# Sample attention with stationary queries, column groups, softmax in halves, and gathered values

## The chip, the core and the metric

The kernel runs on one core of one Trainium2 chip. Its time is the device time of one execution in microseconds (us). TensorE (PE) multiplies; VectorE (DVE), ScalarE (ACT) and GpSimd (POOL) work on tiles; SyncE (SP) issues transfers only, and POOL and ACT issue some too. Each has its own in-order queue, and the queues meet in semaphores.

## What is computed

One layer of a hybrid decoder runs for a prompt of 512 tokens and for a sample group of 8 sequences with one new token each and 2048 tokens behind them. This is the reference of the sample group's attention, which the change rewrites, cut to what matters (B = 8, 8 query heads in 2 key heads of 64, pages of 128 rows, 16 pages to a sequence):

```python
def nsa_sample(a_q, a_kv, a_gate, pool_kc, pool_vc, pool_ks, pool_vs, win_k, win_v, page_table, ...):
    q, (kcr, vcr, ksr, vsr, kwr, vwr) = split_nsa(a_q, a_kv)
    kc = compress(full_rows(pool_kc, kcr), cmp_pe[0], cmp_w1[0], cmp_w2[0])   # 127 rows of 32 tokens
    vc = compress(full_rows(pool_vc, vcr), cmp_pe[1], cmp_w1[1], cmp_w2[1])
    o_cmp, p_grp = cmp_attend(q, kc, vc, q_pos)                  # softmax; p summed over 4 heads
    tok = block_tokens(select_blocks(p_grp, q_pos, PAST_LEN + Q))  # the best 16 of 33 blocks of 64
    o_sel = gathered_attend(q, gather_paged(pool_ks, ...), gather_paged(pool_vs, ...), tok, q_pos)
    o_win = band_attend(q, kw, vw, q_pos, ...)                   # the last 512 rows and the new one
    return combine_branches(a_gate, o_cmp, o_sel, o_win)         # sigmoid gates, sum of three
```

After the three branches the layer computes `merged = sum_b sigmoid(x Wg_b) * (y_b @ w_branch_b)`. Branch 1 of this sum is the attention's.

## The kernel before

The program is a chain of phases: norm, RWKV, mLSTM, prompt attention, sample attention (class `Sample`, from L1603), merge, and feed-forward. All engines meet at a phase's end (`meet`, L247). Everything is fp32, and each matmul in the program is two instructions on TensorE, here called passes. Weights come in pieces of 128 columns through a ring of four (`PIECES`, `weights_in`, L2246); `product` (L238) and `part` (L228) multiply a piece with all 520 tokens.

**One sample.** The 16 pages of a sample lie in one of two buffers, `PG[b % 2]`; a page is 128 x 384 floats: the raw rows of the compressed branch for keys and for values, and the selected branch's keys. SP issues the even pages and POOL the odd ones (`key_pages`), each after reading the page's number into a register. Both wait for the scores of the sample two earlier, `s_sc_ps(b - 2)`, since these were the buffer's last readers. POOL waits for the queries, `qd`, ahead of everything else of the phase; SP fetches samples 0 and 1 a phase ahead. On TensorE the sample is this: L1627 compresses the pages (16 matmuls of 256 columns, 32 passes); L1635 scores the compressed keys of two samples earlier; L1647 shifts and adds the two halves of the blocks of one sample earlier; L1655 scores the selected keys:

```python
for pg in range(NPAGE):
    ins = nc.tensor.matmul(PS[:, 2, pg * 8:pg * 8 + 8], p_[:, pg, 2, :], QD[:, b, :], start=True, stop=True)
```

Here a page's keys are the stationary operand, and the 8 columns of `QD`, one for each head, move. L1659 does the same with the window's keys, and L1669 and L1672 finish the compressed keys and values, `KCs` and `VCs`. VectorE copies all scores into `SC_`, 23 slots of 64 columns (8 samples x 8 heads), with the keys on the partitions.

**After the last sample.** One softmax over all samples follows for the compressed branch (`softmax`, L1676 to L1683 on TensorE: a transpose of the maxima, a broadcast product, a sum), then the ranking of the blocks (L1689, L1692), a mask spread over the keys by 16 products with the constant `BSEL` (L1697), the softmax of the selected and then of the window's scores, and one gate product of the merge (L238). The values come by 128 loads of 64 KB (`value_pages`, L1598) on three queues, SP, POOL and ACT, into six buffers of the then free `PG`; a window's values come on SP. Per sample 23 matmuls (L1713 to L1718) take 8 columns of `SC_` as the stationary operand, and 128 columns of values move. L1722 turns the results back.

**Merge.** For each of 8 output tiles m TensorE computes the attention's gate product (8 matmul pairs) and its branch product (4 pairs), ScalarE the sigmoid, and VectorE the product and the sum. The gate of m = 0 is the one computed inside the sample phase.

Of the kernel before, what the change touches and what calls it, by code (L numbers as in the profile page):

```python
# [20 lines left out]
I32 = mybir.dt.int32  # L21
# [15 lines left out]
RING = 4  # L37
CH = 64
# [8 lines left out]
def constants():  # L47
# [22 lines left out]
    n, j = p[:, None], np.arange(NBLK)[None, :]  # L70
    c["covers"] = ((n < 4 * j + 4) & (n >= 4 * j - 1) & (n < 127)) * 1.0
# [4 lines left out]
    c["first"] = np.zeros((128, 1))  # L76
    c["first"][0] = NEG
# [6 lines left out]


def block_selector():

    e = np.zeros((128, NPAGE, 2, 64))
    for b in range(32):
        e[b, b // 2, b % 2] = 1.0  # L90
    return e.reshape(128, 2048)[0:32].astype(np.float32)
# [62 lines left out]
def build(nc, io, known, phases):  # L154
    ctx = ExitStack()
    with ctx:
# [59 lines left out]
        plan("merge", [8, 4] * 8)  # L216
# [1060 lines left out]
        class Attn:  # L1277
# [245 lines left out]
            def pool(p):  # L1523
# [18 lines left out]
        NSLOT = 23  # L1542
        WIN = [Qr[:, i * 512:(i + 1) * 512] for i in range(2)]
        HIDS = take(512)
        HID, HSGs = HIDS[:, 0:256], HIDS[:, 256:512]
        KCs = take(128)
        QD = take(NS * 8).rearrange("p (b h) -> p b h", b=NS)
        SC_ = take(NSLOT * 64).rearrange("p (s n) -> p s n", s=NSLOT)
        VCs = take(NS * 128).rearrange("p (b f) -> p b f", b=NS)
        MXs, SMs = take(192), take(192)  # L1550
        MXT = take(1)
        DGm = take(192)
        GBs = take(192)
        spent = w1d.rearrange("p kv j l h -> p (kv j l h)")
        ONEW = spent[:, 2048:4096].rearrange("p (k b f) -> p k b f", k=2, b=NS)
        BSEL = spent[:, 0:2048].rearrange("p (g n) -> p g n", g=NPAGE)
        OH = spent[:, 0:1024]
        PGRP = take(16)
        RANK, RSEL = take(NBLK), take(NBLK)
        TOP8 = take(8)  # L1560
        ADDT = take(16)
        ADD = take(256).rearrange("p (g n) -> p g n", g=NPAGE)
        G24D = take(192)
        VPw = [ap.rearrange("p (g f) -> p g f", g=4) for ap in (
            Qr[:, 1024:1536], Qr[:, 1536:2048], KVr[:, 0:512], KVr[:, 512:1024], SGe[:, 0:512], HIDS, *WIN)]
# [6 lines left out]
        VP = [PG[i // 3].rearrange("p g k n -> p (g k n)")[:, i % 3 * 2048:(i % 3 + 1) * 2048].rearrange("p (g f) -> p g f", g=NPAGE)  # L1572
              for i in range(NV)]
        assert a <= TOP - 4680, a
        SLOTS = {"sel": (0, 17), "win": (17, 22), "cmp": (22, 23)}
# [15 lines left out]
        def value_pages(queue, b, lane):  # L1591

            if b < NV:
                queue.wait_ge(*at("s_sc_ps", NS - 2 + b // 3))
            else:
                queue.wait_ge(*at("s_pv", b - NV))
# [4 lines left out]
        HALVES = [[ap[:, :] for ap in ST], [XS[:, :], US[:, :]]]  # L1601

        class Sample:  # L1603
            def pe(pe):

                pe.wait_ge(*at("g24d"))
                ins = nc.tensor.matmul(PS[:, 7, 0:192], C("ones")[0:24, :], G24D[0:24, :], start=True, stop=True)
                ins.then_inc(*step("pe", "gb_ps"))

                for i, kv in enumerate((3, 5)):  # L1610
                    for b in range(NS):
# [816 lines left out]
```

## Time and profile before

| what | value |
|---|---|
| time, median of 3 runs | 1775.79 us (1774.44 to 1775.86) |
| the profiled execution | 1774.47 us, its span 1772.8 us |
| TensorE's mean granted clock | 0.92 |
| PE busy | 1577.5 us, 89% |
| PE weight loads busy | 1305.5 us, 74% |
| DVE, ACT, POOL busy | 682.0, 292.4 and 87.4 us |
| sample phase | 243.2 us (941.2 to 1184.4) |
| its share of one sample | about 18 us, eight times |

The engine that is busy longest is TensorE; the shares say little of one phase, though, since each has limits of its own. The rows that matter are those of the sample phase and of what borders on it: TensorE's timeline with the idle time before each group of instructions and what ended it, the granted clock by stretch, and the transfers' issues. A clock of 1.00 is 2.4 GHz, 0.50 is 1.2 GHz.

### The profile page before, as it was taken

What the parts mean: (1) busy time and instruction counts of PE and PEld (TensorE: products, weight loads), DVE (VectorE), ACT (ScalarE), POOL (GpSimd) and SP (SyncE); (2) the same over time, 40 slices, a digit from 0 to 9 for tenths busy, and PEclk for the clock granted to TensorE, in tenths of its full rate; (3) what the DMA queues carried; (4) which work ended last, traced back from release to release, by engine and by line L of the source; (5) the groups of instructions that cost most, each with busy time, mean ns of one, the idle gap of its engine ahead of it and who ended that gap; (6) DMA issues with size and microseconds to landing.
All of it is one profiled execution on the core that took longest, in us unless ns stands there. A gap on an engine that the chain in (4) does not pass through costs nothing.

```text
span 1772.8 us, 26473 instructions
## 1 busy us (share of the span) xinstructions
PE 1577.5 (89%) x11104; PEld 1305.5 (74%) x11104; DVE 682.0 (38%) x1114; ACT 292.4 (16%) x577; POOL 87.4 (5%) x160
## 2 busy tenths in 40 slices
PE   4996699997888698999998997699988999999993
PEld 3874499886666487777767886478877888888883
DVE  3226855335556503433441102301127545554222
ACT  1013101111321001334431011000011111110000
POOL 0000000000000102000002223000000000000000
PEclk9996799998989596999999786799999999999997
DMA  4220000110211247211105563332222222212301
GB/s 152 72 83 25 25 26 16 40 49 16 72 62 36 77 163 156 67 54 54 48 25 167 184 212 121 111 123 78 84 72 80 95 74 93 96 48 99 121 10 49
DMA packets 57082, 143.35 MB, mean 81 GB/s; under 512 B 12050, under 2 KB 31587, under 8 KB 52835
## 3 DMA queue, kind: packets, MB, share of 16 engines
q1 hardware_dynamic: 36722, 97.01, 16.8%
q0 software_dynamic: 14480, 42.02, 7.7%
q10 hardware_dynamic: 5760, 2.62, 0.5%
q8 instruction: 88, 1.44, 0.3%
q14 instruction: 32, 0.25, 0.0%
HBM read 134.11 MB, written 11.65 MB: 82 GB/s over the span
## 4 chain that ended last, share of the span: by engine, by line
PE 84%; DVE 12%; ACT 1%; issue 1%; DMA 1%; POOL 0%; DVEq 0%; SPq 0%; ACTq 0%; POOLq 0%
PE PS L1982 22%; PE PS L238 20%; PE PS L228 11%; PE PS L1627 4%; PE PS L1234 3%; PE PS L1655 2%; PE PS L1713 2%; PE PS L1379 1%; PE PS L254 1%; PE PS L1374 1%; PE PS L1342 1%; PE PS L524 1%; PE PS L536 1%; PE PS L537 1%; PE PS L989 1%
## 5 line engine op out<-in xcount | busy, mean ns | idle before, releaser
L238 PE MATMUL PS<-xyr 128*128 128x260 f32 x1184 | 268.0, 389 | 4.0 <-DVE arena L825 2.5
L238 PEld LDWEIGHTS PS<-xyr 128*128 128x128 f32 x1184 | 228.7, 194 | 40.6 <-DVE arena L825 2.9
L228 PE MATMUL PS<-xyr 128*128 128x260 f32 x896 | 215.3, 393 | 11.0 <-DVE xyr L301 5.8
L228 PEld LDWEIGHTS PS<-xyr 128*128 128x128 f32 x896 | 169.4, 194 | 48.1 <-DVE xyr L301 6.6
L1982 PE MATMUL PS<-arena 128*128 128x260 f32 x638 | 145.1, 383 | 1.5 <-DVE arena L2140 1.3
L1982 PEld LDWEIGHTS PS<-arena 128*128 128x128 f32 x638 | 120.9, 190 | 21.5 <-DVE arena L2140 1.7
L1982 PE MATMUL PS<-xyr 128*128 128x260 f32 x512 | 119.2, 382 | 0.0
L1982 PE MATMUL PS<-arena,xyr 128*128 128x260 f32 x484 | 110.3, 382 | 0.0
L1982 PEld LDWEIGHTS PS<-xyr 128*128 128x128 f32 x512 | 97.3, 190 | 14.9
L1982 PEld LDWEIGHTS PS<-arena,xyr 128*128 128x128 f32 x484 | 92.0, 190 | 14.1
L238 PE MATMUL PS<-arena,xyr 128*128 128x260 f32 x384 | 87.4, 388 | 2.2 <-DVE arena L1920 1.6
L238 PEld LDWEIGHTS PS<-arena,xyr 128*128 128x128 f32 x384 | 73.9, 193 | 14.2 <-DVE arena L1920 2.0
L1627 PE MATMUL PS<-arena 128*128 128x256 f32 x256 | 71.8, 449 | 2.4 <-DVE arena L1769 2.4
L1627 PEld LDWEIGHTS PS<-arena 128*128 128x128 f32 x256 | 58.3, 231 | 13.7 <-DVE arena L1769 2.7
L1520 DVE COPY arena<-PS 128x512 f32<-128x512 f32 x20 | 13.8, 692 | 82.7 <-PE PS L1374 82.7
L2152 DVE TENSOR_TENSOR arena<-PS,arena 128x260 f32<-128x260 f32 x22 | 9.4, 429 | 92.6 <-ACT arena L2082 92.6
L1401 ACT ACTIVATE arena<-PS,arena 128x128 f32<-128x128 f32 (+3 forms) x64 | 32.9, 527 | 56.2 <-DVE arena L1485 56.1
L1982 PE MATMUL PS<-xyr,arena 128*128 128x260 f32 x176 | 42.2, 382 | 0.0
L683 DVE TENSOR_TENSOR arena<-arena 128x512 f32<-128x512 f32 x14 | 9.7, 693 | 76.8 <-ACT arena L601 76.8
L1588 POOL DMA_DIRECT2D arena<-in_pages x64 | 34.4, 538 | 88.2 <-issue 88.2
L537 PE MATMUL PS<-arena 64*64 64x64 f32 x640 | 37.8, 218 | 0.0
L536 PE MATMUL PS<-arena 64*64 64x64 f32 x640 | 37.8, 218 | 0.0
(478 smaller groups left out, 2190.9 us busy)
## 6 DMA issues: line engine op xcount, KB each, us to landing
xyr<-in_w SPq DMA_DIRECT2D x73, 512.0 KB, 3.5
xyr<-in_w_up SPq DMA_DIRECT2D x22, 1024.0 KB, 4.9
arena<-in_pages SPq DMA_DIRECT2D x64, 192.0 KB, 3.6
arena<-in_pages POOLq DMA_DIRECT2D x64, 192.0 KB, 3.8
xyr<-in_w_down SPq DMA_DIRECT2D x10, 704.0 KB, 8.0
xyr<-in_w SPq DMA_DIRECT2D x24, 256.0 KB, 2.7
arena<-in_w_down SPq DMA_DIRECT2D x6, 704.0 KB, 6.0
arena<-in_x POOLq DMA_DIRECT2D x2, 2080.0 KB, 8.6
```

The lines of the kernel that those rows point to most:

```text
L228: ins = nc.tensor.matmul(PS[:, 2 * bank + half, 0:HALF], weight(g, k), XN[:, k, half * HALF:(half + 1) * HALF], start=k == 0, stop=k == KT ...
L238: ins = nc.tensor.matmul(PS[:, 2 * bank + half, 0:HALF], weight(g, k), src[:, k0 + k, half * HALF:(half + 1) * HALF], start=first and k == ...
L254: ins = nc.tensor.matmul(PS[:, 2 * t + half, 0:HALF], C(which), src[:, t, half * HALF:(half + 1) * HALF], start=True, stop=True)
L536: nc.tensor.matmul(PS[q, 4 + g // 8, g % 8 * 64:g % 8 * 64 + 64], TTt[q, g, :], Wt[q, g, :], start=True, stop=True)
L537: ins = nc.tensor.matmul(PS[q, g // 8, g % 8 * 64:g % 8 * 64 + 64], Wt[q, g, :], TTt[q, g, :], start=True, stop=True)
L1234: ins = nc.tensor.matmul(PS[:, 2 * FILL + half, 0:HALF], weight(g, k), src[:, k, half * HALF:(half + 1) * HALF], start=k == 0, stop=k == 3)
L1401: nc.scalar.activation(Pb[i % 2][:, x, 0:W], PS[:, x, 0:W], ACT.Exp, bias=NBi[i % 2][:, x:x + 1], scale=SCALE, accum_out=SUMi[i % 2][:, x: ...
L1588: queue.dma_start(PG[b % 2][:, pg], io["pages"][page(queue, b, pg)].rearrange("a p k n -> p (a k) n")).then_inc(*moved("pages", b, lane, l ...
L1627: ins = nc.tensor.matmul(PS[:, kv, 0:256], w1[:, kv, l, :, :].rearrange("p j h -> p (j h)"), p_[:, :, kv, l * 16:(l + 1) * 16], start=l == ...
L1655: ins = nc.tensor.matmul(PS[:, 2, pg * 8:pg * 8 + 8], p_[:, pg, 2, :], QD[:, b, :], start=True, stop=True)
L1713: nc.tensor.matmul(out, SC_[:, pg, o], VP[b % NV][:, pg, :], start=pg == 0, stop=False)
L1982: ins = nc.tensor.matmul(dst, w[:, k, :], src[:, k, :], start=first and k == 0, stop=k == n - 1, skip_group_check=not first)
```

## The change

It rewrites the sample phase and takes three gates of the merge into it.

- **Queries.** `QZ` holds for each sample 32 columns that are zero but for the 8 heads of its place in its half (samples 0 to 3, 4 to 7). They are the stationary operand now, and the keys move: four products of 512 columns (L1723), each into a column group of its own, partitions 32c to 32c + 31 of the result. The four samples of a half add up in one bank, so that after four samples the 128 partitions hold all scores of the half: 4 page groups x 4 samples x 8 heads. The window (L1727) and the compressed keys (L1661) go the same way.
- **Compressed rows.** Block-diagonal weights `W2B` make keys and values in one product each (L1653, L1654). The new row of a branch is written into column 0 of the window's and the compressed keys, so that no product has a single row. Halves are shifted and added in the same sample (L1737).
- **Softmax in halves.** A row lies on four partitions now, and constants (`mod32`, `rep4`) join them. Half 0 is worked out during samples 4 to 7, a step in the middle or behind a page product each; half 1 between gates and values. VectorE's 32 x 32 block transposes turn the probabilities into the stationary operand `PT` of the value products.
- **Values.** `PT` has 32 columns, the values move in four column groups (L1674). One indirect gather on POOL brings a sample's 16 value pages (1 MB, 128 rows of 2048 floats); the 128 row numbers are worked out on VectorE from a table that POOL loads first. The window's values are loaded on SP between the key pages. ScalarE copies each sample's result and TensorE adds the four groups (L1684).
- **Gates.** The gate products m = 0, 1, 2 stand in the sample phase, cut into parts (`gate_part`), and ScalarE keeps their sigmoids in `GATED`.
- **Constants** are 160 columns wider, and `blocksel` is gone.

```diff
+AHEAD = 3
...
-        plan("merge", [8, 4] * 8)
+        plan("gates", [8] * AHEAD)
+        plan("merge", [4] * AHEAD + [8, 4] * (8 - AHEAD))
...
             if b >= 2:
                 queue.wait_ge(*at("s_sc_ps", b - 2))
-                queue.wait_ge(*at("s_hid_ps", b - 2))
...
-            for pg in (range(0, 6), range(6, 11), range(11, NPAGE))[lane]:
-                queue.dma_start(VP[b % NV][:, pg], io["pages_v"][page(queue, b, pg)].rearrange("a p n -> p (a n)")).then_inc(
-                    *moved("pages_v", b, lane, lane=NV * lane + b % NV))
+            p.indirect_dma_start(VP[b % NV], None, io["pages_v"], bass.IndirectOffsetOnAxis(ap=IDX[:, b:b + 1], axis=0)).then_inc(
+                *moved("pages_v", b, lane=b % NV))
...
+                    for i in range(NPAGE):
+                        c = i % 4
+                        nc.tensor.matmul(PS[32 * c:32 * c + 32, bank_, 0:128], PT[hf][:, i * 32:i * 32 + 32],
+                                         VP[b % NV][:, i * 128:i * 128 + 128], start=i < 4, stop=False)
+                    for c in range(3, -1, -1):
+                        nc.tensor.matmul(PS[32 * c:32 * c + 32, bank_, 0:128], PTw[hf][:, 32 * c:32 * c + 32], VPw[b][:, c, :],
+                                         start=False, stop=c > 0)
+                    ins = nc.tensor.matmul(PS[0:32, bank_, 0:128], PTc[hf], VCs[:, b, :], start=False, stop=True)
...
+                        pe.wait_ge(*at("qd"))
+                    if b in at_b:
+                        at_b[b](0)
+                    if b >= 1:
+                        compressed(b - 1)
+                    hf = b // 4
+                    for c in range(4):
+                        ins = nc.tensor.matmul(PS[32 * c:32 * c + 32, 1 + hf, :], QZ[:, b, :], p_[:, 4 * c:4 * c + 4, 2, :],
+                                               start=b % 4 == 0, stop=b % 4 == 3)
+                    pe.wait_ge(*at("s_new_k", b))
+                    for c in range(4):
+                        ins = nc.tensor.matmul(PS[32 * c:32 * c + 32, 3 + 4 * hf, 0:128], QZ[:, b, :], WIN[b % 2][:, c * 128:(c + 1) * 128],
+                                               start=b % 4 == 0, stop=b % 4 == 3)
+                    ins.then_inc(*step("pe", "s_sc_ps", b))
...
+                v.wait_ge(*at("table_rows"))
+                nc.vector.tensor_copy(TVF, TVI).then_inc(*step("dve"))
...
+                    nc.vector.transpose(PT[hf].rearrange("p (i r) -> p i r", i=NPAGE), SM[:, 0:512].rearrange("p (x i) -> p i x", i=NPAGE)).then_inc(*step("dve"))
...
-                p.dma_start(BSEL[0:32].rearrange("p g n -> p (g n)"), io["blocksel"]).then_inc(*moved("blocksel"))
+                p.dma_start(TVI, io["table_rows"]).then_inc(*moved("table_rows"))
                 p.wait_ge(*at("qd"))
...
+                p.wait_ge(*at("value_rows"))
                 for b in range(NS):
-                    value_pages(p, b, 1)
+                    value_pages(p, b)
...
+                    if b >= 2:
+                        for x in range(b - 2, b - 1 if b < NS - 1 else NS):
+                            sp.dma_start(VPw[x], io["win_v"][:, x]).then_inc(*moved("windows_v", x, lane=x))
+                for g in range(start["gates"], start["gates"] + RING):
                     weights_in(g)
-                for b in range(NS):
-                    value_pages(sp, b, 0)
```

On TensorE one sample in the middle of the loop reads so before (line, operation, result and operands, rows x columns of the moving operand, count, and the semaphores that it waits for):

```order
L1635 MATMUL PS<-arena 127x8 [waits dve_steps]
L1647 MATMUL PS<-rwkv_x,cn 64x127 [waits act_steps]
L1647 MATMUL PS<-rwkv_x,cn 64x127 x3
L1647 MATMUL PS<-rwkv_u,cn 64x127 x4
L1655 MATMUL PS<-arena 128x8 [waits dve_steps]
L1655 MATMUL PS<-arena 128x8 x15
L1656 MATMUL PS<-arena 1x8
L1659 MATMUL PS<-arena 128x8 [waits moved_win0]
L1659 MATMUL PS<-arena 128x8 x3
L1660 MATMUL PS<-arena 1x8
L1669 MATMUL PS<-arena 64x127 [waits dve_steps]
```

and so after the change, from the end of one page product to the end of the sample:

```order
L1699 MATMUL PS<-arena 128x256 x15
L1653 MATMUL PS<-arena 128x128 [waits dve_steps]
L1654 MATMUL PS<-arena 128x128
L1655 MATMUL PS<-cn,arena 1x128
L1723 MATMUL PS<-arena 32x512 x4
L1727 MATMUL PS<-arena 32x128 [waits dve_steps]
L1727 MATMUL PS<-arena 32x128 x3
L1737 MATMUL PS<-rwkv_state,cn 64x127 [waits act_steps]
L1737 MATMUL PS<-rwkv_state,cn 64x127 x7
L1661 MATMUL PS<-arena 32x128 [waits dve_steps]
```

The sixteen products of 8 columns have become four of 512, and the step that waits for ScalarE's copy of the halves now stands behind the scores.

On TensorE the end of the phase reads so before, from the ranked blocks to the first value product (L1713; the softmax steps wait for VectorE one by one):

```order
L1692 MATMUL PS<-cn,arena 32x16 [waits dve_steps]
L1697 MATMUL PS<-arena 128x16 [waits moved_blocksel,dve_steps]
L1697 MATMUL PS<-arena 128x16 x15
L1677 MATMUL PS<-cn,arena 64x128 [waits dve_steps]
L1680 MATMUL PS<-arena,cn 128x64 [waits dve_steps]
L1683 MATMUL PS<-arena,cn 128x64 [waits dve_steps]
L1677 MATMUL PS<-cn,arena 64x128 [waits dve_steps]
L1680 MATMUL PS<-arena,cn 128x64 [waits dve_steps]
L1683 MATMUL PS<-arena,cn 128x64 [waits dve_steps]
L238 MATMUL PS<-xyr 128x260 [waits moved_weights1]
L238 MATMUL PS<-xyr 128x260 x15
L1713 MATMUL PS<-arena 8x128 [waits moved_pages_v6,moved_pages_v12,moved_pages_v0,moved_windows_v0,dve_steps]
```

and so after, from the second part of gate 0 to the first value product (L223 is `part` with a gate's weights, L1674 the values of sample 0):

```order
L223 MATMUL PS<-xyr 128x260 [waits moved_weights1]
L223 MATMUL PS<-xyr 128x260 x7
L1661 MATMUL PS<-arena 32x128 [waits dve_steps]
L223 MATMUL PS<-xyr 128x260 [waits moved_weights2,act_steps]
L223 MATMUL PS<-xyr 128x260 x7
L1613 MATMUL PS<-cn,arena 128x32 [waits dve_steps]
L223 MATMUL PS<-xyr 128x260 [waits moved_weights2]
L223 MATMUL PS<-xyr 128x260 x3
L1618 MATMUL PS<-cn,arena 8x33 [waits dve_steps]
L223 MATMUL PS<-xyr 128x260 [waits moved_weights2]
L223 MATMUL PS<-xyr 128x260 x3
L1674 MATMUL PS<-arena 32x128 [waits dve_steps,moved_pages_v0]
```

Between steps that wait for VectorE there stand parts of gate products now, and the values of sample 0 come before half 1 has its mask.

On POOL the end of the queue reads so before, with one register load, address and transfer for each page of values:

```order
L1580 TENSOR_LOAD arena
L1580 ISA x2
L1598 ISA
L1598 DMA arena<-in_pages_v 128x128
L1931 DMA arena<-in_x 128x4160 [waits pool_steps,phase_left]
```

and so after, from the last page of keys on (in_pages_v is the table of value rows):

```order
L1577 TENSOR_LOAD arena
L1577 ISA x2
L1584 ISA
L1584 DMA arena<-in_pages 128x384
L1994 DMA arena<-in_win 128x512 [waits pe_steps]
L1593 DMA arena<-in_pages_v,arena 128x2048 [waits pe_steps,dve_steps]
L1593 DMA arena<-in_pages_v,arena 128x2048 [waits pe_steps] x7
L2061 DMA arena<-in_x 128x4160 [waits pool_steps,phase_left]
```

Eight gathers stand in the place of the value pages, the first three behind TensorE's scores of sample 6.

## Rows read from the trace of the kernel before

**Rows 1.** The page: the span, and TensorE's granted clock in 40 slices.

```profile
span 1772.8 us, 26473 instructions
...
PEclk9996799998989596999999786799999999999997
```

**Rows 2.** Stretches of the sample phase; after POOL's column: clock, DMA share, GB/s.

```profile
979.00:997.00 18.00, 17.05 (x104) 14.95 (x102) 1.51 (x8) 1.79 (x6) 4.83 (x9) 0.78 0.59 190
1110.50:1129.50 19.00, 3.36 (x10) 2.21 (x11) 12.69 (x18) 1.58 (x2) 0.00 (x0) 0.50 0.35 102
1129.50:1138.40 8.90, 8.90 (x34) 7.21 (x33) 1.28 (x3) 0.00 (x0) 0.00 (x0) 0.80 0.33 98
1144.00:1160.00 16.00, 16.00 (x139) 11.21 (x137) 0.00 (x0) 1.28 (x1) 5.37 (x10) 1.00 0.58 164
941.20:1184.40 243.20, 204.54 (x1292) 168.53 (x1292) 37.44 (x119) 18.71 (x53) 56.44 (x105) 0.79 0.50 157
```

**Rows 3.** TensorE's timeline over one sample: start, duration, engine, line, operation, [idle before].

```profile
979.04 9.06 PE L1627 MATMUL PS<-arena 128*128 128x256 f32 x32
...
989.22 3.74 PE L1655 MATMUL PS<-arena 128*128 128x8 f32 x32
...
993.01 1.79 PE L1659 MATMUL PS<-arena 128*128 128x8 f32 x8
...
995.87 0.69 PE L1669 MATMUL PS<-arena 64*64 64x127 f32 x4 [0.94 <-DVE arena L1785]
...
997.11 8.56 PE L1627 MATMUL PS<-arena 128*128 128x256 f32 x32
```

**Rows 4.** TensorE's timeline: the phase's entry, its tail, and the merge behind it.

```profile
948.19 8.86 PE L1627 MATMUL PS<-arena 128*128 128x256 f32 x32 [2.37 <-DVE arena L1769]
...
1093.88 0.59 PE L1635 MATMUL PS<-arena 128*127 128x8 f32 x2 [0.66 <-DVE arena L1789]
...
1103.25 7.00 PE L1697 MATMUL PS<-arena 32*128 32x16 f32 x32 [0.32 <-DVE arena L1846]
...
1138.45 3.66 PE L1713 MATMUL PS<-arena 128*8 128x128 f32 x32
...
1184.42 5.37 PE L238 MATMUL PS<-arena,xyr 128*128 128x260 f32 x16 [0.56 <-DVEq L247]
...
1189.63 7.18 PE L238 MATMUL PS<-xyr 128*128 128x260 f32 x32
...
1196.65 3.67 PE L238 MATMUL PS<-arena,xyr 128*128 128x260 f32 x16
```

**Rows 5.** TensorE's timeline: products in groups of half width or half height.

```profile
678.57 0.46 PE L1321 MATMUL PS<-arena 64*32 64x64 f32 x16
...
930.81 0.65 PE L1379 MATMUL PS<-arena 128*64 128x256 f32 x4
...
931.39 0.66 PE L1374 MATMUL PS<-cn,arena 128*128 128x128 f32 x4
...
970.49 1.14 PE L1647 MATMUL PS<-rwkv_state,cn 128*64 128x127 f32 x16
```

**Rows 6.** POOL's timeline: the first window, first and last page of one sample.

```profile
944.08 0.59 POOL L1873 DMA_DIRECT2D arena<-in_win  x1 [2.06 <-DVE arena L1765]
...
962.96 0.54 POOL L1588 DMA_DIRECT2D arena<-in_pages  x1 [8.63 <-issue]
...
971.26 0.54 POOL L1588 DMA_DIRECT2D arena<-in_pages  x1 [0.61 <-issue]
```

**Rows 7.** DMA issues of the sample phase: count, KB each, median us to landing.

```profile
arena<-in_pages POOLq DMA_DIRECT2D x56, 192.0 KB, 3.8
...
arena<-in_blocksel POOLq DMA_DIRECT2D x1, 256.0 KB, 3.5
```

**Rows 8.** ScalarE's timeline, the last sample's end: a table load.

```profile
1091.42 1.28 ACT L1746 ACT_TABLE_LOAD   x1
```

**Rows 9.** VectorE's timeline: its longest strided step in the softmax.

```profile
1113.02 1.97 DVE L1799 TENSOR_REDUCE arena<-arena 128x64 f32<-128x1088 f32 x1
```

More of the change, by code:

```diff
@@ L1552, in build @@
[L1552 to L1563 removed]
+        QZr = take(288)
@@ L1571, in build @@
         NV = 6
[L1572 to L1575, printed above, removed]
+        VP = [PG[i // 3].rearrange("p g k n -> p (g k n)")[:, i % 3 * 2048:(i % 3 + 1) * 2048] for i in range(NV)]
+        MOD = C("mod32")
         def page(queue, b, pg):
@@ new lines, in gate_part @@
+                def gate_part(m, ks):
+                    if ks[0] == 0:
+                        if m:
+                            pe.wait_ge(*at("gate_sig", m - 1))
+                        else:
+                            pe.wait_ge(*at("s_x", NS - 1))
+                    part(pe, start["gates"] + m, 0, ks)
+                gate_part(0, range(0, 4))
+                compressed(NS - 1)
+                gate_part(0, range(4, 8))
+                cmp_scores(NS - 1)
+                gate_part(1, range(0, 4))
@@ new lines, in pe @@
+                pattern(1)
+                gate_part(1, range(4, 6))
+                rank(1)
+                gate_part(1, range(6, 8))
+                values(0)
+                mask(1)
+                values(1)
+                heads(0)
+                values(2)
+                heads(1)
+                max_rows(1)
+                values(3)
+                heads(2)
+                max_columns(1)
+                heads(3)
+                gate_part(2, range(0, 2))
+                sums(1)
@@ new lines, in exp_all, with gate_out @@
+                def exp_all(hf):
+                    act.wait_ge(*at("c_nb2", hf))
+                    nc.scalar.activation(SM, SM, ACT.Exp, bias=NB2[:, 0:1], scale=SCALE, accum_out=SUM2[:, 0:1]).then_inc(*step("act"))
+                    nc.scalar.activation(SW, win_ps(hf), ACT.Exp, bias=NB2[:, 1:2], scale=SCALE,
+                                         accum_out=SUM2[:, 1:2]).then_inc(*step("act", "c_exp2", hf))
+                def gate_out(m):
+                    act.wait_ge(*at("tile", start["gates"] + m))
+                    nc.scalar.activation(halves(GATED[m]), pair(0), ACT.Sigmoid).then_inc(*step("act", "gate_sig", m))
@@ new lines, in dve @@
+                for b in range(NS):
+                    r, n = 32 * (b % 4), b // 4 * 128
+                    v.wait_ge(*at("windows_v", b))
+                    nc.vector.tensor_copy(VPw[b][0:1, 0, :], NVW[r:r + 1, n:n + 128]).then_inc(*step("dve", "new_w", b))
+                compressed(NS - 1)
+                cmp_weights(1)
+                group(1)
+                top(1)
+                masked(1)
+                max_all(1)
+                bias(1)
+                normalise(1)
+                weights_w(1)
@@ L1885, in build, with gate, branch_piece, gate_piece @@
         assert a < TOP - 4680
+        def gate(m):
+            return GATED[m] if m < AHEAD else SG[m % 2]
+        def branch_piece(m):
+            return start["merge"] + (m if m < AHEAD else 2 * m - AHEAD + 1)
+        def gate_piece(m):
+            return start["gates"] + m if m < AHEAD else branch_piece(m) - 1
         class Merge:
@@ L1906, in act @@
             def act(act):
-                for m in range(8):
-                    act.wait_ge(*at("tile", start["merge"] + 2 * m))
-                    if m >= 2:
+                for m in range(AHEAD, 8):
+                    act.wait_ge(*at("tile", gate_piece(m)))
+                    if m >= AHEAD + 2:
                         act.wait_ge(*at("gated", m - 2))
-                    nc.scalar.activation(halves(SG[m % 2]), pair(m % 2), ACT.Sigmoid).then_inc(*step("act", "gate_sig", m))
+                    nc.scalar.activation(halves(gate(m)), pair(m % 2), ACT.Sigmoid).then_inc(*step("act", "gate_sig", m))
                 squares_act(act, "norm2", X2, SQ2t, range(KT), "x2")
@@ L2263, in _ @@
             up_weights(0)
-            for g in range(start["merge"] + RING, len(PIECES)):
+            for g in range(start["gates"] + RING, len(PIECES)):
                 weights_in(g)
```

573 lines of the change are left out of this document (312 added, 261 removed).

## The prediction

> **What bounds the kernel now.** I read the page first: the span, and the granted clock of TensorE, which dips over slices 23 to 26 of 40 [rows 1]. Then the stretches of that place: the sample phase takes 243.2 us (941.2 to 1184.4) at a mean clock of 0.79, and inside it one stretch stands at 0.50 and another at 1.00 [rows 2]. Then TensorE's timeline. One sample lasts 18.1 us (979.04 to 997.11): the page product 9.1; sixteen scores whose keys are the stationary operand and whose moving operand has 8 columns, 3.7; the window's, 1.8; then 0.94 of waiting for VectorE ahead of the last small products [rows 3]. At full clock 32 passes of 260 columns take 7.02 us (1189.63 to 1196.65), 0.219 a pass, so a page product of 32 passes of 256 is worth 6.9 [rows 4]; it takes 8.6 to 9.1 [rows 3]. Each sample thus loses about 2 us to the lower level, which follows the stretch of 8-column scores. Pages don't bound it: the product at 997.11 waits for nothing.
>
> After the last sample (1093.88) come 35 us of softmax and ranking, in which TensorE is busy for 3.4 of 19 us at clock 0.50 [rows 2] and spends 7.0 on sixteen tiny products [rows 4]; then a gate product, 8.9 at 0.80 [rows 2]; eight value products of 23 matmuls, 46 passes at 0.114, 5.3 us each [rows 4]; and two small steps. All of it is one chain. So three prices count: TensorE's work per sample, what follows the last sample, and, new, how fast pages come.
>
> **Entry.** Before, the first page product starts 7.0 us into the phase (948.19), behind VectorE's preparation and transposes of the new values [rows 4]. After, it is TensorE's first instruction, and its pages were fetched a phase ahead: 0.3. But POOL fetches nothing more until the padded queries are there, and VectorE now makes them behind a small table that POOL loads first; every VectorE step of the phase is queued behind that wait. Before, the queries released POOL at 944.08, 2.9 us in [rows 6]; a small POOL load takes up to 3.5 to land [rows 7]; with some ten small operations I put the release at 5.3. Then the window, eight page issues at 1.19 (962.96 to 971.26, seven steps [rows 6]) and 3.8 until the last has landed [rows 7]: sample 1 has its pages at about 18.5, where TensorE was done with sample 0 at 12.3. It waits 6 us and then runs a product partly at half clock, 2 us.
>
> **One sample.** TensorE: page product 6.9; three products of 128 columns (6 passes of 0.11) 0.65; the scores, 2048 key columns in four column groups. A 512-column product is two passes of 0.43, 0.86: one after the other the four take 3.4, side by side 0.9. No row shows four groups of full height. The nearest: two groups of 64 columns send sixteen 127-column passes in 1.14 us, where one after the other they need 1.7; four passes of 256 columns take 0.58 (930.81 to 931.39), where serial is 0.86 and side by side 0.43; eight tiles of 64 x 32 send sixteen 64-column passes in 0.46 against 0.85 [rows 5]. All three lie at side by side, with 0.15 for the change of form (0.58 less 0.43). I take 0.9, and 0.2 for the window, 1.1 for the halves as now, 0.2 for the compressed scores, four changes 0.6: 10.5 in all, 9.0 up to the end of the scores.
>
> The Trainium skill (TensorE: Matmul & The Clock Gate, Part 3: Packing small matmuls — row/col tiling) reports 2.38 times for three column groups, not 3. By that factor, an estimate, the scores would take 1.4 and a value product 2.0 where I take 1.2; the sum would be 6 us higher, since the scores would still end under the page loads. Rows 5 reach nearer to the full factor; no row has four groups of full height.
>
> Pages: two buffers remain, and a load starts when the scores of two samples earlier are done. From there to the last landing: one step of 1.2 to the first issue, 8.3 of issues, 3.8 to land, 13.3 [rows 6, 7]. Two samples thus take at least 9.0 + 13.3 = 22.3, 11.2 each, above TensorE's 10.5: **the next limit is the issue of pages on POOL and SP**. SP also carries a window's values between two sets of pages now, and these share the DMA engines; I take 11.5. Samples 2 to 7: 69. With 18.5 for the first and 12.5 for sample 1 the loop ends at 100 us, against 1094.5 - 941.2 = 153.3: **53 less**. Half 0's softmax lies under samples 4 to 7, each step beside a 6.9 us product. ScalarE changes its table between Exp and Sigmoid eight times at 1.28 [rows 8]; behind such products it costs nothing, uncovered 10. The first gate's weights follow the last pages and windows on SP, issued at about 87 and due at 100: nothing, unless the loop gets shorter by ten.
>
> **After the loop.** Three gates of 7.0: 21.0. Half 1's softmax stands in program order between gate pieces and the values of half 0; it is covered if each step takes under 2 us. VectorE's block transposes have no row: between one small step and its longest strided pass, 2.0 [rows 9], and 2.6 of gate stands over them. I count 2 for this chain's own small products and 1.5 for waits (the second gate needs ScalarE to empty the first's banks). Value products: 21 matmuls, 42 passes of 128 columns; serial 4.8, side by side 0.65 to stream plus filling and waits. I take 1.2, eight times 9.6. Heads: eight at 0.35, 2.8. Compressed leftovers 1, changes of form 1, exit 1. **40**, where before had 1184.4 - 1094.5 = 89.9: 50 less.
>
> Values now come by eight gathers of 1 MB on POOL instead of 128 loads on three queues. No row shows a gather. Lower bound: one issue and one landing of 128 rows, 0.5 + 3.8 [rows 6, 7]; upper: the sixteen issues that it replaces, at 1.19, 19 us. The form is the former's, one instruction of 128 rows, with more bytes to a row; I take 6. Three may start when sample 6's scores are done (about 87) and stand at 105; the first value product is due at 117. The next three stand by 123 and are needed from 121 on, each 1.6 later; the last two have a gate more. Covered, nearly.
>
> The Trainium skill (DMA: Bandwidth & Descriptors, Bandwidth) gives 6.15 us for a 1 MB load from GpSimd; by that figure the sum stays as it is.
>
> **After the phase.** Two of the merge's middle gates are gone from it: 14.0 less (two stretches like 1189.63 to 1196.65 [rows 4]). Constants are 160 columns, 82 KB, wider ahead of the first step: +0.3.
>
> **Sum.** Phase 243.2 to 140, -103; merge -14; start +0.3: -117. The profiled run took 1774.5 (span 1772.8 [rows 1]), so 1657.5; the median of the runs is 1.3 above it, which gives **1659**.
>
> **Rivals.**
> - *Groups one after the other.* Scores 3.4 + 0.9: TensorE 13.7 a sample, 2.2 above the pages, +15; values 4.8, +29: 1703. Overlap by half only: +10, 1669. For it: rows 5 show half width or half height only; against it: all three pairs overlap. 15% for both.
> - *The clock stays low.* If the waits for pages bring back the lower level, a product is 8.8 again [rows 3], a sample 12.4: +7, and half the gates and values slower, +15: 1681. Against it: value products with 8 stationary columns ran at 1.00 through 1144 to 1160; for it: the broken-up stretch at 0.50 [rows 2]. 15%.
> - *A slow gather.* At 10 us each the eight stand at 167 and not before 139: +28, 1687. 8%.
> - *Slower than before.* The same mechanism further on: POOL works out 128 row addresses one by one. To lose the 117 the eight must end at 257, 21 us each from 87 on, just above the bound of sixteen issues. 4%, 1 of it even.
> - *The loop doesn't shorten:* pages keep arriving every 18 us because the DMA engines, not the late start, set their pace: 6 x 6.6 = 40 more, 1699. Against it: before, a load is done 12.1 us after its first issue (962.96 to 971.26, and 3.8 [rows 6, 7]). 3%.
>
> **Numbers.** The forecast has 55% (1648 to 1670). The range takes in the low clock, half overlap and the slow gather, and at the low end a loop at TensorE's own 10.5 and values at 0.9: **1640 to 1695**. Outside are serial groups, 6%, late pages, slower, and 5% of the forecast's own ends. About 0.2% (3.5 us) can be told from no change: faster 0.96, within 0.01, slower 0.03.
>
> **What would show it.** Page products at 6.9 and a clock of 1.00 between samples; four score groups within 1.1 us; a period of 11 to 12 us ended by a page load, not by VectorE; a wait of some 6 us ahead of sample 1; no idle time over 1 us from the first gate on; gathers that land in 4 to 8 us; a merge 14 us shorter. Wrong: four groups in 2 us or more, a gather above 10, table loads that TensorE waits for.

## The result

The changed kernel takes 1661.17 us (median of 4 runs, 1658.19 to 1664.79) against 1775.19 (4 runs, 1774.44 to 1775.86): a ratio of 0.9359, with an interval of 0.9334 to 0.9384. Forecast was 1659, range 1640 to 1695. Run again beside later experiments it took 1662.38, ratio 0.9356 (0.9340 to 0.9372). The profiled execution took 1663.99, at the upper end of the four.

The page after, its span and TensorE's granted clock, against [rows 1]:

```profile
span 1662.3 us, 25262 instructions
...
PEclk9997699999889869699999979999989999999997
```

The dip of slices 23 to 26 is gone; a smaller one at 24 is left. TensorE's timeline (start, duration, engine, line, operation, idle time before and what ended it) over the loop and the tail, against [rows 3, 4]:

```profile
940.96 7.17 PE L1699 MATMUL PS<-arena 128*128 128x256 f32 x32 [1.00 <-DVEq L242]
...
949.00 1.04 PE L1723 MATMUL PS<-arena 128*32 128x512 f32 x8
...
960.45 9.73 PE L1699 MATMUL PS<-arena 128*128 128x256 f32 x32 [7.66 <-issue]
...
973.29 7.17 PE L1699 MATMUL PS<-arena 128*128 128x256 f32 x32
...
986.97 10.12 PE L1699 MATMUL PS<-arena 128*128 128x256 f32 x32 [3.32 <-DMA arena<-in_pages]
...
1000.20 7.17 PE L1699 MATMUL PS<-arena 128*128 128x256 f32 x32
...
1014.18 6.71 PE L1699 MATMUL PS<-arena 128*128 128x256 f32 x16 [3.62 <-DMA arena<-in_pages]
...
1042.52 3.69 PE L1699 MATMUL PS<-arena 128*128 128x256 f32 x16 [2.08 <-issue]
...
1053.15 3.77 PE L223 MATMUL PS<-xyr 128*128 128x260 f32 x16
...
1070.01 1.08 PE L1674 MATMUL PS<-arena 128*32 128x128 f32 x32
1070.91 0.40 PE L1677 MATMUL PS<-arena 128*32 128x128 f32 x8
...
1071.61 1.08 PE L1674 MATMUL PS<-arena 128*32 128x128 f32 x32
...
1093.21 10.79 PE L233 MATMUL PS<-arena,xyr 128*128 128x260 f32 x48 [0.56 <-DVEq L242]
...
1103.84 7.18 PE L233 MATMUL PS<-xyr 128*128 128x260 f32 x32
```

Stretches of the same phase (length, busy time of five engines, then clock, DMA share, GB/s), against [rows 2]:

```profile
960.45:965.20 4.75, 4.75 (x11) 3.83 (x12) 0.15 (x1) 0.00 (x0) 1.99 (x5) 0.50 1.05 379
965.20:970.00 4.80, 4.80 (x22) 4.14 (x21) 0.00 (x0) 0.00 (x0) 0.94 (x2) 0.95 0.54 181
973.29:980.30 7.01, 7.01 (x33) 6.19 (x33) 0.49 (x2) 0.92 (x4) 3.35 (x7) 1.00 0.86 263
986.97:992.00 5.03, 5.03 (x12) 4.04 (x13) 0.15 (x1) 0.00 (x0) 2.56 (x5) 0.50 1.05 379
1042.52:1049.90 7.38, 7.38 (x34) 6.24 (x35) 2.92 (x10) 0.00 (x0) 0.73 (x1) 1.00 1.04 420
939.96:1053.15 113.19, 93.44 (x657) 73.36 (x656) 19.89 (x89) 20.69 (x56) 38.73 (x69) 0.89 0.80 270
1053.15:1093.20 40.05, 38.94 (x480) 31.52 (x479) 10.84 (x46) 11.60 (x25) 3.75 (x4) 1.00 0.52 204
```

Four column groups of scores take 1.04 us (949.00) where sixteen products took 3.74: the first four passes start within 0.03 us, the next four 0.43 later. The page product takes 7.17 when TensorE comes to it without a wait or behind one of 1.0 (940.96, 973.29, 1000.20) and 9.7 to 10.1 behind waits of 7.7 and 3.3 (960.45, 986.97); there its first 5 us stand at 0.50, the lower level. The same holds for the first half of sample 5's, 6.71 behind 3.6 (1014.18). Sample 7's stands at 1.00 behind a wait of 2.1, with a DMA share as high as that of the slow ones (1042.52). Sixteen value products take 1.08 instead of 3.66. From the first gate on (1053.15) the clock is 1.00, and no wait exceeds 0.4 up to the phase's end. The merge begins with three branch products in a row (1093.21, 48 passes), and its first gate is that of m = 3 (1103.84): five are left there of seven.

By stretches, from the profiles of before and after:

| | forecast | measured |
|---|---|---|
| start of the phase | +0.3 | -1.2 (941.2 to 939.96) |
| loop, from the phase's start | 100 | 113.2 (to 1053.15) |
| tail, to the first merge product | 40 | 40.1 (to 1093.21) |
| phase | -103 | -90.0 (243.2 to 153.2) |
| merge's gates and branches | -14 | -15.6 (80.6 to 65.0) |
| all that follows | 0 | -3.7 (507.8 to 504.1) |
| span | -117 | -110.5 |

The start of the phase is no effect of the change that one could read: the first page product began anywhere from 939.8 to 944.2 in thirteen profiles whose earlier phases are alike. Of the 3.7 behind the merge there is one profile before; the later ones have 502 to 505. Whether chance or not stays open.

### The profile page after: what moved, and what is told of

Read it like the earlier page. It is cut to its first block, busy times and chain, and to the rows that moved or that the text cites. A ratio compares the mean times of both kernels' runs of the same rounds, so it can differ in the third digit from the quotient of the medians.

```text
span 1662.3 us, 25262 instructions
## 1 busy us (share of the span) xinstructions
PE 1489.3 (90%) x10882; PEld 1228.6 (74%) x10882; DVE 674.1 (41%) x1128; ACT 303.5 (18%) x600; POOL 73.5 (4%) x128
## 4 chain that ended last, share of the span: by engine, by line
PE 82%; DVE 10%; issue 2%; DMA 2%; ACT 2%; SPq 1%; POOL 0%; DVEq 0%; ACTq 0%; POOLq 0%
PE PS L2112 23%; PE PS L233 20%; PE PS L223 13%; PE PS L1229 3%; PE PS L1699 2%; PE PS L1374 1%; PE PS L249 1%; PE PS L1369 1%; PE PS L1337 1%; PE PS L519 1%; PE PS L531 1%; PE PS L532 1%; DMA arena<-in_pages 1%; PE PS L984 1%; DVE arena L692 1%
## 5 line engine op out<-in xcount | busy, mean ns | idle before, releaser
L223 PE MATMUL PS<-xyr 128*128 128x260 f32 x992 | 238.7, 393 | 11.1 <-DVE xyr L296 5.8
L223 PEld LDWEIGHTS PS<-xyr 128*128 128x128 f32 x992 | 187.2, 194 | 51.6 <-DVE xyr L296 6.6
L2112 PEld LDWEIGHTS PS<-arena 128*128 128x128 f32 x638 | 120.9, 190 | 21.3 <-DVE arena L2270 1.7
L2112 PEld LDWEIGHTS PS<-xyr 128*128 128x128 f32 x512 | 97.3, 190 | 14.9
L2112 PEld LDWEIGHTS PS<-arena,xyr 128*128 128x128 f32 x484 | 92.0, 190 | 14.1
L1699 PE MATMUL PS<-arena 128*128 128x256 f32 x256 | 66.6, 423 | 17.7 <-issue 9.7
L1699 PEld LDWEIGHTS PS<-arena 128*128 128x128 f32 x256 | 53.8, 214 | 27.9 <-issue 10.4
L532 PEld LDWEIGHTS PS<-arena 64*64 64x64 f32 x640 | 37.4, 135 | 0.0
```

Source lines behind the costliest of these rows:

```text
L223: ins = nc.tensor.matmul(PS[:, 2 * bank + half, 0:HALF], weight(g, k), XN[:, k, half * HALF:(half + 1) * HALF], start=k == 0, stop=k == KT ...
L532: ins = nc.tensor.matmul(PS[q, g // 8, g % 8 * 64:g % 8 * 64 + 64], Wt[q, g, :], TTt[q, g, :], start=True, stop=True)
L1699: ins = nc.tensor.matmul(PS[:, 0, kv * 256:kv * 256 + 256], w1[:, kv, l, :, :].rearrange("p j h -> p (j h)"), p_[:, :, kv, l * 16:(l + 1) ...
L2112: ins = nc.tensor.matmul(dst, w[:, k, :], src[:, k, :], start=first and k == 0, stop=k == n - 1, skip_group_check=not first)
```

## Experiments

Each is one edit of the changed kernel, but for the last three, which put several together. Times are to be held against its 1661 and 1662, ratios against 0.9359 and 0.9356.

**The kernel again.**

> The changed kernel itself, beside the three below on one chip. Its four runs were 1658.2, 1658.4, 1664.0 and 1664.8; expected between 1657 and 1666, with the page products of samples 1, 3 and 5 at 9.5 us or more again.

1662.38, ratio 0.9356. Samples 1, 3 and 5 waited 7.2, 3.1 and 3.7 us, and the products behind these waits were slow again, 9.9, 8.6 and 9.1, two of them below the 9.5 expected. Sample 7's was slow in its first half too (5.38 behind 2.65). Single profiles differ by some us in the loop: from the first page product to the first gate it takes 112.2, 111.1, 109.2 and 110.7 in this kernel's two profiles and in those of two later runs that leave the loop as it is.

**Value products one group after the other.**

```diff
-                        c = i % 4
+                        c = i // 4
...
```

> The sixteen value products of a sample are reordered so that four successive ones go to the same column group instead of four different ones; the sums are the same. Theory (neighbouring products in different column groups run side by side): the group of 32 passes, 1.08 us in the trace after the change, takes 3.66 as it did with 8 stationary columns before; 2.7 more for each of eight samples, all on the chain that ends the phase: 22 us more, about 1683. Rival (a pass with 32 stationary columns is short by itself, and its neighbour doesn't matter): no change, 1661.

1672.81, ratio 0.9427 (0.9412 to 0.9443). TensorE's timeline of one sample's values:

```profile
1068.21 2.35 PE L1674 MATMUL PS<-arena 128*32 128x128 f32 x31
```

The 32 passes take 2.35 where they took 1.08 and, with 8 stationary columns, 3.66 [rows 4]: the order alone costs 1.3 a sample, and the tail grew from 40.1 to 49.9. So neighbours in different groups do run side by side. The size of the theory was wrong: this order isn't serial either. The value products that start in the first 0.4 us show it, here, in the changed kernel and in the kernel before:

```profile
1068.21 0.62 PE L1674 MATMUL PS<-arena 128*32 128x128 f32 x4
...
1070.01 0.64 PE L1674 MATMUL PS<-arena 128*32 128x128 f32 x16
...
1138.45 0.60 PE L1713 MATMUL PS<-arena 128*8 128x128 f32 x4
```

The first four passes, all of one group, start 0.11 apart, as in the kernel before; then two start every 0.11 us, until the last four stand alone again: 20 steps of 0.11. So a pass with 32 stationary columns is no shorter by itself, which was the rival, and the factor of 4 comes from the groups.

**Waits filled with products that nobody reads.**

```diff
+                    for i in range((0, 16, 0, 8, 0, 8, 0, 8)[b]):
+                        nc.tensor.matmul(PS[:, 0, 0:256], w1[:, 0, 0, :, :]..., XN[:, 0, 0:256], start=True, stop=True)
                     for lane in range(2):
                         pe.wait_ge(*at("pages", b, lane))
```

> TensorE fills its waits for pages with products that nobody reads: 16 of them (7 us) ahead of sample 1, 8 (3.5 us) ahead of samples 3, 5 and 7. Theory (the waits bring the lower clock, the slow page product behind each wait delays the scores that release the next pages, so the loss feeds itself): page products of samples 1, 3, 5 at 7.2 us instead of 9.7, 10.1 and 10.4, the loop about 8 us shorter, about 1653. Rival (the DMA engines set the pace of the loop, whatever TensorE does): the products are as fast, but the waits grow by as much; within 2 us of 1661. Second rival (the clock doesn't follow TensorE's idle time): products stay at 10, 1661 or up to 3 more.

1656.42, ratio 0.9328 (0.9313 to 0.9344; the end of that interval touches the changed kernel's). The timeline shows what the ratio barely does:

```profile
953.75 7.17 PE L1694 MATMUL PS<-xyr,arena 128*128 128x256 f32 x32
...
960.95 7.14 PE L1702 MATMUL PS<-arena 128*128 128x256 f32 x32
...
981.50 3.72 PE L1694 MATMUL PS<-xyr,arena 128*128 128x256 f32 x16
...
985.06 7.07 PE L1702 MATMUL PS<-arena 128*128 128x256 f32 x32
```

and so does the stretch of the whole loop:

```profile
942.00:1046.59 104.59, 102.14 (x735) 82.42 (x736) 19.05 (x87) 20.32 (x55) 38.73 (x69) 1.00 0.88 298
```

The products of samples 1 and 3 take 7.1, the clock is 1.00 through the loop, and the loop ends 5 to 8 us earlier (104.6 from the first page product, where four profiles have 109.2 to 112.2), although TensorE does some 18 us of products for nothing (953.75, and three like 981.50). DMA share and GB/s are higher than before, not lower. So the lower level followed TensorE's waits and not the busy DMA engines. That the loss feeds itself, as the theory has it, isn't shown: sample 3's pages take 14.1 us from first issue to last landing in both kernels, and the wait that the idle products cover there is still 3.3 (981.5 to the last landing at 984.8). A slow product moves the next release by what it loses itself, and no more.

**Four pages ahead of the queries.**

```diff
+                key_pages(p, 1, 1, range(1, 9, 2))
                 p.wait_ge(*at("qd"))
```

> POOL fetches four of its eight pages of sample 1 before it waits for the queries. Theory (the wait of 7.7 us ahead of sample 1 is POOL's wait for the queries): the last page of sample 1 lands some 5 us earlier, the wait falls to 2 to 3 us and the whole loop moves up by 5, about 1656. Rival (the pages come at the DMA engines' pace): the landing moves by less than 2 us, or later waits take it back, 1659 to 1661.

1657.70, ratio 0.9334 (0.9318 to 0.9349). The wait ahead of sample 1 fell from 7.7 to 3.4 us, and the loop, from the first page product to the end of the last, from 109.1 and 108.0 to 102.7. The theory's 5 holds within what single profiles differ by (five with the changed kernel's loop have 106.0 to 109.1); the interval of the ratio overlaps the changed kernel's.

```profile
956.63 9.56 PE L1699 MATMUL PS<-arena 128*128 128x256 f32 x32 [3.44 <-DMA arena<-in_pages]
```

**Queries ahead of the row numbers.** VectorE's steps on the table `TVI` move behind the queries.

> VectorE makes the padded queries first and works out the row numbers of the values behind them, so that the queries don't wait for POOL's small table. Theory (POOL's wait for the queries, of which the table's 2.4 us are a part, holds the pages of sample 1): POOL's first window goes out some 2.5 us earlier, the first window's scores no longer wait 1.3, the loop moves up by 2 to 2.5: 1656 to 1659 where the changed kernel stands at 1658 to 1665. Rival (the four block copies set when the queries are there, not the table): less than 1 us.

1656.96, ratio 0.9323 (0.9305 to 0.9340). POOL's timeline, the table and the first window:

```profile
940.07 0.58 POOL L1987 DMA_DIRECT2D arena<-in_table_rows  x1 [224.94 <-DVEq L242]
...
941.45 0.55 POOL L1994 DMA_DIRECT2D arena<-in_win  x1 [0.79 <-DVE arena L1847]
```

TensorE's, the first window's scores and sample 1:

```profile
950.19 0.42 PE L1727 MATMUL PS<-arena 128*32 128x128 f32 x8 [1.30 <-DVE arena L1947]
...
954.88 9.97 PE L1699 MATMUL PS<-arena 128*128 128x256 f32 x32 [3.25 <-issue]
```

The window goes out 1.4 us behind the table's issue; it was 4.6 (941.23 and 945.88). The wait ahead of sample 1 is 3.3, and the time lies where the theory put it (against the changed kernel run beside it, the intervals touch). So most of POOL's wait was for the table, through VectorE's queue. The 1.30 ahead of the first window's scores did not move: the theory had put it down to the same wait, but what precedes it on VectorE are four copies of the new values' rows, 1.77 us.

**A third queue for pages.**

```diff
-            for pg in range(lane, NPAGE, 2):
+            for pg in range(lane, NPAGE, 2 if b == 0 else 3):
```

with `key_pages(act, b + 2, 2)` behind ScalarE's steps of each sample.

> From sample 1 on ScalarE's queue issues five of the sixteen pages, SP six and POOL five. Theory (the issue of pages on two queues sets the pace): the last issue of a sample comes 2.3 to 3 us earlier, so does the last landing, and the waits of samples 1, 3, 5 and 7 shrink by as much: 8 to 11 us less, about 1652. Rival (the DMA engines are full, their share stood at 1.05 behind each wait): pages take as much longer to land as they are issued earlier, 0 to 3 us less, 1658 to 1661.

1650.11, ratio 0.9297 (0.9282 to 0.9313). Page issues from sample 3's on (count, KB, median us to landing), the changed kernel and then this one:

```profile
arena<-in_pages SPq DMA_DIRECT2D x40, 192.0 KB, 4.5
...
arena<-in_pages POOLq DMA_DIRECT2D x40, 192.0 KB, 4.6
```

```profile
arena<-in_pages SPq DMA_DIRECT2D x30, 192.0 KB, 5.5
...
arena<-in_pages POOLq DMA_DIRECT2D x25, 192.0 KB, 5.4
...
arena<-in_pages ACTq DMA_DIRECT2D x25, 192.0 KB, 5.5
```

Two samples in the middle of the loop of this kernel:

```profile
966.96:987.10 20.14, 17.92 (x111) 15.00 (x111) 1.62 (x7) 3.06 (x12) 6.39 (x12) 1.00 0.99 333
```

Each half is half right. The sixteen pages of sample 3 were issued in 6.1 us instead of 8.5, yet landed 13.0 us after the first issue instead of 14.1: with a DMA share of 0.99 the rest went into landing. The 11 us came from sample 1, whose pages ScalarE could ask for without the queries (wait 1.9), and from shorter waits: sample 3's product kept 7.17 behind 2.2 us.

**Two thirds of the bytes.** The page loads of samples 2 to 7 leave the selected keys out, so the scores of these samples use older keys.

> From sample 2 on a page load leaves out the selected branch's keys: 128 KB instead of 192, as many loads; the scores of samples 2 to 7 are those of older keys. Theory (issue and a landing of its own): first issue to last landing falls from 14.1 us to no less than 12, eight steps of 1.15 and 3.5; the loop 5 to 7 shorter, 1653 to 1657. Rival (bytes): two thirds of 14.1 is 9.4, TensorE then never waits behind sample 1, the loop 15 to 20 shorter, 1643. If bytes don't matter at all: 1661.

1653.54 (2 runs), ratio 0.9309 (0.9288 to 0.9330). First issue to last landing of sample 3: 12.2 us (973.94 to 986.19), as the issue theory says, while a page landed in 3.0 instead of 4.5. With two queues the issue holds the larger part and the bytes the last 2 us. The loop shortened to 100.9, by 8 to 11, more than the 5 to 7 expected, since no product from sample 2 on was slow; this is sample 3's:

```profile
986.28 7.14 PE L1700 MATMUL PS<-arena 128*128 128x256 f32 x32 [1.48 <-issue]
```

**No gates in the sample phase.** `AHEAD = 0`, no `gate_part`.

> No gate of the merge in the sample phase: the eight gates are all in the merge. Theory (the three gates cover the softmax of half 1, which is a chain of some twenty small steps on VectorE and ScalarE): the merge gets 21 longer, the tail loses 21.6 of gates, but the chain stands open, 15 to 25 us, and the value products behind it run at the lower clock: about 1680 to 1688. Rival (the chain fits beside the values of half 0): 0 to 5 more, 1661 to 1666.

1677.55, ratio 0.9426 (0.9400 to 0.9452). The longest waits of TensorE in that tail, and the last:

```profile
1056.86 0.49 PE L1653 MATMUL PS<-arena 128*128 128x128 f32 x2 [1.36 <-DVE arena L1949]
...
1059.56 0.41 PE L1661 MATMUL PS<-arena 128*32 128x128 f32 x2 [1.68 <-DVE arena L1932]
...
1061.49 0.31 PE L1613 MATMUL PS<-cn,arena 32*128 32x32 f32 x1 [1.52 <-DVE arena L1865]
...
1076.36 1.94 PE L1674 MATMUL PS<-arena 128*32 128x128 f32 x32 [1.11 <-DVE arena L1924]
```

The merge got 21.05 longer (86.0), the tail 9 shorter instead of 21: some 12 us stood open, 8.4 of it waits and 2.6 value products at 1.94 instead of 1.08 behind them. Less than expected, since much of half 1's chain lies beside the values of half 0: TensorE works on them from 1062.2 to 1072.1 without a wait. Three gates cost 9 us in the tail and 21 in the merge.

**The gather undone.**

```diff
-            p.indirect_dma_start(VP[b % NV], None, io["pages_v"], ...IDX[:, b:b + 1]...)
+            for pg in range(lane, NPAGE, 2):
+                p.dma_start(VP[b % NV][8 * pg:8 * pg + 8, :], rows[page(p, b, pg)]...)
```

> The gather is undone: a sample's sixteen value pages come by sixteen loads of 64 KB into 8 partitions each, eight issued by POOL and eight by SP. Theory (the gather is worth the issue of these loads): eight issues of 1.15 us for each sample, from 1039 us on, the last sample's at 1039 + 74 + 4 = 1117 where its products stand at 1090: 25 to 30 more, about 1688. Rival (the DMA engines, not the issue, set when the values are there): within 5 us of 1661.

1703.57, ratio 0.9585 (0.9556 to 0.9613). TensorE's timeline over the last samples' values:

```profile
1086.14 1.94 PE L1677 MATMUL PS<-arena 128*32 128x128 f32 x32 [10.67 <-DMA arena<-in_pages_v]
...
1107.46 1.93 PE L1677 MATMUL PS<-arena 128*32 128x128 f32 x32 [6.58 <-issue]
...
1127.81 1.93 PE L1677 MATMUL PS<-arena 128*32 128x128 f32 x32 [7.09 <-issue]
```

Ten us a sample, not 9.2: SP needs 1.3 for each of these steps, its last goes out at 1125.1, and the products behind the waits are slow as well (1.93). It costs more than either expectation: by time the gather is worth 42 us here, by the ratios 40.

**Gates where TensorE waits.** Three more gates, ahead of samples 1, 3 and 7, into banks that are free there.

```diff
+                    if b in INLOOP:
+                        ...
+                                ins = nc.tensor.matmul(PS[:, banks[half], 0:HALF], weight(g, k), XN[:, k, half * HALF:(half + 1) * HALF],
+                                                       start=k == 0, stop=k == KT - 1)
```

> Three more gates of the merge are computed in the sample phase, ahead of samples 1, 3 and 7, where TensorE waits for pages (7.7, 3.3 and 2.1 us); the three in the tail stay. Theory (those waits are idle time of TensorE, and filling them keeps the clock up): the merge loses three stretches of 7.0, 21 less; in the loop the gate ahead of sample 1 costs nothing and gives back 2.5 of its slow product, the one ahead of sample 3 costs 7.2 less 3.3 and 3.0, the one ahead of sample 7 costs 5: about 18 less in all, 1643. Rival (the gates' weights, 1.5 MB more in the loop, hold the pages up and push the waits behind the gates): each gate's weights cost 2 us of page loads, 8 to 12 less, about 1650.

1653.23, ratio 0.9295 (0.9271 to 0.9319): a gain of 8 us by time and of 11 by the ratio (the kernel before took 1778.63 beside it), as the rival has it, where the theory had 18. TensorE's timeline at the first of these gates:

```profile
957.22 10.00 PE L1702 MATMUL PS<-xyr 128*128 128x260 f32 x32 [3.94 <-DMA xyr<-in_w]
```

The first gate's weights came behind sample 1's pages on SP, so it waited 3.9 for them and ran slow, 10.0: it held sample 1 up by 6 instead of filling its wait. The wait ahead of sample 5 grew too, from 3.6 to 5.2.

**The same with the third queue.**

> The three gates ahead of samples 1, 3 and 7, and pages issued from three queues from sample 1 on. Theory (gates fill TensorE's waits, and pages land earlier): the loop is then bound by TensorE, eight samples of 10.3 and three gates of 7.2, 104 us, with at most 4 us of waits where no gate stands; merge 21 less: 1630. Rival (the DMA engines bound the loop: sixteen pages take 13.0 us from first issue to last landing on three queues too, and the gates' weights come on top): the loop at 113, 1640.

1645.08, ratio 0.9249 (0.9223 to 0.9274); above both expectations, and nearest to the rival (1640; by the ratio it is 1642). TensorE's timeline at the first gate and ahead of sample 5:

```profile
956.80 8.76 PE L1702 MATMUL PS<-xyr 128*128 128x260 f32 x32 [2.52 <-DMA xyr<-in_w]
...
1016.37 3.69 PE L1713 MATMUL PS<-arena 128*128 128x256 f32 x16 [2.85 <-DMA arena<-in_pages]
```

From the phase's start to the first gate of the tail it takes 117 us, with 23.3 of gates in it, longer than both had it; the wait for weights (2.5, and 8.8 for the gate behind it), one of 1.9 for the first window and one of 2.9 ahead of sample 5 are left. Behind this last one the half product is not slow, 3.69, while one of no_gates_ahead takes 5.38 behind 1.9 (1043.11): the length of a wait alone doesn't tell whether the product behind it is slow.

**The same with the weights first, the queries first, and eight idle products ahead of sample 5.**

> The three gates ahead of samples 1, 3 and 7 and the third queue as before, and besides: the first gate's weights are loaded ahead of sample 1's pages, VectorE makes the queries first, and eight products that nobody reads stand ahead of sample 5. Theory (in the kernel with gates and third queue the wait of 2.5 for weights, the slow gate behind it, the 1.9 at the first window and the 2.9 ahead of sample 5 are what is left in the loop): 2.5 + 1.6, 1 to 2, and 2 to 3 less: 1637 to 1639. Rival (the DMA engines are full through the whole loop, a load that goes earlier delays another): 1642 to 1645.

1641.16 (5 runs, 1639.77 to 1641.74), ratio 0.9237 (0.9223 to 0.9251): the fastest, 20 to 21 us below the changed kernel.

```profile
952.58 7.28 PE L1703 MATMUL PS<-xyr 128*128 128x260 f32 x32
...
959.70 7.07 PE L1717 MATMUL PS<-arena 128*128 128x256 f32 x32
```

```profile
940.83:1052.57 111.74, 109.16 (x768) 88.48 (x768) 18.92 (x87) 22.32 (x61) 27.47 (x48) 1.00 0.86 304
```

TensorE is busy for 109.2 of 111.7 us at 1.00, with three gates and 3.7 us of idle products among it. The theory was 2 to 4 too low, and the rival's 1642 too high: 1.3 at the first window stayed, and the idle products ahead of sample 5 cost more than the 2.9 they replaced. What bounds this loop is TensorE.

## Why the prediction held

The forecast of 1659 is near the 1661 for the right reasons in the tail. That the sum fits so closely is partly luck: the loop was 13 us too short in it, and half of that was made up elsewhere.

- **One sample on TensorE: right.** Page product 7.17 for 6.9; scores 1.04 for 0.9; 10.3 from 973.29 to the next sample's turn at about 983.6, forecast 10.5. The rival of groups one after the other is out: the 32 passes of a value product start within 0.90 us in the trace (from 1070.01 to the first pass of the next line), where before it was 3.59, from 1138.45 [rows 4] to this pass of its next line, a factor of 4:

```profile
1142.04 0.38 PE L1714 MATMUL PS<-arena 1*8 1x128 f32 x2
```

The Trainium skill (TensorE: Matmul & The Clock Gate, Part 3: Packing small matmuls — row/col tiling) has 2.38 for three groups; this trace has the full factor for four.
- **The next limit: right in kind, short in size.** It is the pages, as forecast, and the waits stand ahead of every other sample. The failed term is "two samples thus take at least 9.0 + 13.3 = 22.3", rounded up to 11.5 a sample. Measured from the end of sample 1's scores to the end of sample 3's (972.0 to 998.9) it is 26.9: 14.9 to the last landing, because the last pages, which share the DMA engines with two window loads and the first pages of the next sample, land in 5.6 and not 3.8, and 11.9 for the product and scores, because the product behind a wait took 10 and not 6.9. The prediction had this second effect as a rival, "the clock stays low", and put it at 15%; it charged it to sample 1 alone in its own sum. The rival came true for samples 1, 3 and 5, in some profiles for 7, not for gates and values. A clock of 1.00 between samples was one of the signs that the prediction named for itself; it did not show. Six samples took 79.9 instead of 69.
- **Sample 1: right within 2 us.** 7.7 of wait and 2.6 of slow product, forecast 6 and 2. That POOL's wait for the queries is its cause is shown by two runs, and that the table is most of it by one.
- **The tail: right**, 40.1 for 40. Gates of 7.2, a sample's values and heads at 1.75 (from 1071.61 to the next) for 1.55, waits 0.5 for 1.5. ScalarE loads its table eight times, as forecast; behind none of them does TensorE wait more than 0.8.
- **The gather: right in effect, not in size.** Landings took 5.7 to 15.0, median 10.4:

```profile
arena<-in_pages_v,arena POOLq DMA_INDIRECT x8, 10.4
```

But POOL spends only about 1 us on each, three are under way at once, and the first three land 3.5 and 3.9 apart (1049.9, 1053.4, 1057.3), well ahead of 1070. A gather above 10 was one of the prediction's signs of being wrong; it came true and cost nothing. The price of the rival "a slow gather", eight times 10 one after the other, is out: what counts is that they overlap. The figure of the Trainium skill (DMA: Bandwidth & Descriptors, Bandwidth) for 1 MB from GpSimd, 6.15, is close to the 5.7 of the gather issued at 1071.78, with one other beside it; the others took 7.6 to 15.0.
- **After the phase:** two gates, 14.0, as forecast, and 1.6 more, since the merge's first branch product takes 3.6 now and took 5.37 at less than full clock [rows 4].

So the loop came out 13 longer than forecast, the rest 6.7 shorter, 3.7 of these unexplained: the profiled run is some 6 above the forecast for it; the median of the runs is 2.8 below that run.

## What to carry to other kernels

Where a transfer is released by the product that it waits behind, add up the whole circle, and take the product at the speed it has after a wait, not at its best. Work that is due anyway is the best filling for such waits, and its weights have to be ahead of the data that cause the wait. A small load that an engine waits for at the head of its queue holds all that is queued behind it, so what others wait for goes first.

## What was not expected of the hardware

- Column groups reach the full factor of four: eight passes of 512 columns in four groups in 1.04 us, 32 of 128 in 1.08. In an order that keeps four products in one group the 32 still take 2.35, not 3.66.
- Products whose results nobody reads made the loop faster: 18 us of them, 5 to 8 us less, while the granted clock stays at 1.00, 2.4 GHz.
- Three gathers of 1 MB under way at once took 10.2, 12.4 and 15.0 us to land, 3.5 and 3.9 apart; POOL was busy for 1 us with each. Sixteen loads of 64 KB took 10 us of issue on two queues.
